# w2 read as four neighbouring rows to a partition, and the hidden activations turned with a stride of four

## The chip, the cores and the metric

The kernel runs on one core of one Trainium2 chip. The metric is the device time of one execution in microseconds (us), lower is better. The core's engines are TensorE (PE; its weight loads are listed apart as PEld), VectorE (DVE), ScalarE (ACT), GpSimd (POOL) and SyncE (SP), which here only issues transfers; 16 DMA engines move data between HBM and the on-chip memory SBUF. TensorE writes its results into PSUM.

## The reference, cut to what matters

The program is one decoder layer: attention and gated linear attention share a projection, then comes a mixture of experts, then a gated per-layer embedding. The change lies in the mixture of experts alone, for 512 tokens with 1024 features, 32 experts, 4 experts a token:

```python
def clamped_swiglu(hid):
    x_glu = jnp.minimum(hid[..., ::2], SWIGLU_LIMIT)
    x_lin = jnp.clip(hid[..., 1::2], -SWIGLU_LIMIT, SWIGLU_LIMIT)
    return x_glu * jax.nn.sigmoid(SWIGLU_ALPHA * x_glu) * (x_lin + 1.0)
...
    def expert_block(args):
        xb, e = args
        hid = xb @ w1[e] + b1[e]                    # 1024 -> 2048
        return clamped_swiglu(hid) @ w2[e] + b2[e]  # 1024 -> 1024
```

The second product is a sum over the 1024 hidden features. A sum can be taken in any order, so row f of `w2` only has to meet column f of the activations; on which partition and in which step of the sum they meet is free.

## The kernel before, in words

The expert part is a loop over 32 blocks, one for each expert with up to 96 token rows (`CAP`); in these inputs no expert needs a further block. All of w1 and w2 of an expert (12 MB) is streamed from HBM in 12 chunks of 1 MB, each 128 partitions by 2048 numbers. Chunks 0 to 3 and 6 to 9 are w1, chunks 10 and 11 are the first half of w2 (hidden features 0 to 511), and chunks 4 and 5 are the second half of the w2 of the expert before. SP issues the loads (L370) into a ring of six slots; the load of a chunk is issued once DVE has finished with the chunk six places ahead of it.

Each chunk goes through three engines. ACT rounds it to the upper part (`split_hi`, L703), DVE makes the rest, chunk minus upper part (`split_lo`, L1398), and both parts go to `HL`, a ring of four. PE then multiplies (w1 at L1063, w2 at L1091): for each of the chunk's two 128-row pieces it does three products (upper activations by upper weights, upper by rest, rest by upper), each in two halves of 512 columns, so 12 matmuls a chunk and 144 a block. The activations are what is loaded into the PE array, the weights of the model stream past.

Between the products DVE and ACT form the SwiGLU result `HIDr` (96 token rows by 1024 features, written by L1419 in two halves). PE turns each half in `turn_hidden` (L1098): four transposes, in each of which a 96 x 128 piece of `HIDr` is the array's load and the 96 x 96 identity streams past. The result is 128 features by 96 tokens. ACT copies it (L733, `HIDTh`) and DVE makes its rest (L1423, `HIDTl`); L1091 then uses piece f of `HIDTh` with piece f of w2. PE takes its work in a fixed order: chunks 0, 1, turn the second half of the block before, chunk 2, turn the next tokens (`turn_x`, L1051), chunk 3, bias, chunks 4, 5, then chunks 6, 7, turn the first half, chunks 8, 9, biases (L1072, L1079), chunks 10, 11.

Of the kernel before, what the change touches and what calls it, by code (L numbers as in the profile page):

```python
# [14 lines left out]
P = 128  # L15
# [12 lines left out]
CAP = 96  # L28
# [9 lines left out]
WRING = 6  # L38
# [4 lines left out]
def hybrid_layer(nc, x, p, g_mix, w_in, w_gla_gate, b_gla_gate, g_gla_norm, w_out, g_ffn, w_router, b_router,  # L43
                 w1, b1, w2, b2, w_ple_gate, w_ple_proj, g_ple, g_final, out):
    ctx = ExitStack()
    with ctx:
        def sb(name, shape, dt=F32):
            return ctx.enter_context(nc.sbuf_tensor(name, shape, dt))

        def sem(name):  # L50
            return ctx.enter_context(nc.semaphore(name))
# [6 lines left out]
        def scope(*shapes):  # L58

            with ExitStack() as held_here:  # L60
                return [held_here.enter_context(nc.sbuf_tensor(name, shape, dt)) for name, shape, dt in shapes]
# [9 lines left out]
        def in_w(at, *shape):  # L71
# [32 lines left out]
        ident = sb("ident", [P, P])  # L104
# [70 lines left out]
        BB, HIDr, HIDTh, HIDTl, T1, T2, SIG, _, XG, XTh, XTl, sel, _, W45 = scope(  # L175
            ("BB", [2 * NE, 3 * D], F32R),
            ("HIDr", [CAP, D], F32),
            ("HIDTh", [P, NC, CAP], F32R), ("HIDTl", [P, NC, CAP], F32R),
            ("T1", [CAP, 512], F32), ("T2", [CAP, 512], F32), ("SIG", [CAP, 512], F32),
            ("skip4", [P, 256], F32),  # L180
            ("XG", [CAP, D], F32),
            ("XTh", [P, NC, CAP], F32R), ("XTl", [P, NC, CAP], F32R),
            ("sel", [2 * NE, CAP], F32R),
# [3 lines left out]
        def w_slot(k):  # L187
            s = k % WRING
            return W[:, s * 2048:(s + 1) * 2048] if s < 4 else W45[:, s - 4]
# [8 lines left out]
        ps = ctx.enter_context(nc.psum_tensor("ps", [P, 8, 512], F32))  # L198
# [8 lines left out]
        w_in_s = [sem(f"w_slot_in{s}") for s in range(WRING)]  # L207
# [154 lines left out]

        def load_chunk(sp, b, k, e):
            if k in (4, 5, 10, 11):
                f = 512 + 256 * (k - 4) if k < 6 else 256 * (k - 10)
                src = w2[0, bass.ds(e, 1), f:f + 256, :]
            else:
                c, n = 256 * (k % 6), 1024 * (k // 6)
                src = w1[0, bass.ds(e, 1), c:c + 256, n:n + 1024]
            sp.dma_start(w_slot(k).rearrange("p (c n) -> p c n", c=2),  # L370
                         src.rearrange("o (c p) n -> p (o c) n", p=P)).then_inc(w_in_s[k % WRING], 16)

        def load_expert(sp, b, e, before_e):
            for k in range(NK):
                sp.wait_ge(w_lo, b * NK + (k - 7))
                load_chunk(sp, b, k, before_e if k in (4, 5) else e)

        def extra_blocks(eng, body):

            n = eng.value_load(tab[0:1, NEXTRA + 1:NEXTRA + 2], min_val=0, max_val=NEXTRA)  # L380
            with eng.If(n > 0):
                with eng.Fori(0, n) as i:
                    body(i)
            return n
# [4 lines left out]
        def _(sp):  # L389
# [28 lines left out]
            for k in range(4):  # L418
                load_chunk(sp, 0, k, 0)
# [3 lines left out]
            for k in range(6, 10):  # L423
                sp.wait_ge(w_lo, k - 5)
                load_chunk(sp, 0, k, 0)
# [409 lines left out]
        def _(pe):  # L835
# [4 lines left out]
            for c in range(NC):  # L840
                if c >= 4:
                    pe.wait_ge(at_lo, c - 3)
                for t in range(NT):
                    if c == 0:
                        pe.wait_ge(xs_ready, t + 1)
                    last = pe.transpose(ps[:, c % 4, t * P:(t + 1) * P], xs[:, t, c * P:(c + 1) * P], ident[:])
# [18 lines left out]
            for i, (name, _) in enumerate(CH):  # L865
                if name == "v":

                    pe.wait_ge(kt_ready, 2)
                    for hp in range(2):
                        g = GRP["ktok"] + hp  # L870
                        pe.wait_ge(proj_out, g - 3)
                        for t in range(NT):
                            last = pe.transpose(ps[:, g % 4, t * P:(t + 1) * P], ktail[:, hp, t * P:(t + 1) * P], ident[:])
                        last.then_inc(proj, 1)
                    pe.wait_ge(proj_out, GRP["ktok"] + 2)
                    for c in range(7):
                        t, r = c // 2, GC * (c % 2)
                        bank, at = 4 + c % 2 + 2 * (t // 2), 256 * (t % 2)
                        for h in range(GH):
                            lo = 64 * (h % 2)  # L880
                            last = pe.matmul(ps[lo:lo + 64, bank, at + (h // 2) * P:at + (h // 2 + 1) * P],
                                             ktok[r:r + GC, t, h * 64:(h + 1) * 64], vg[r:r + GC, t, h * P:(h + 1) * P],
                                             start=True, stop=True)
                        last.then_inc(kv_done, 1)
                for j in range(4):
                    g = GRP[name] + j
                    pe.wait_ge(proj_out, g - 3)
                    for c in range(NC):
# [8 lines left out]
                        for m, (l, r) in enumerate(pairs):  # L897
                            last = pe.matmul(ps[:, g % 4], l, r, start=(c == 0 and m == 0), stop=(c == NC - 1 and m == 2))  # L898
# [41 lines left out]
            for t in range(NT):  # L940
# [6 lines left out]
                for h in range(GH):  # L947
                    last = pe.matmul(ps[:, 1, h * P:(h + 1) * P], kd[:, h // 2, tt], qz[:, h, tt], start=True, stop=True)
                last.then_inc(a_done, 1)
                for i in range(MH + 2):  # L950
# [12 lines left out]
                    if 1 <= i <= MH:  # L963
# [5 lines left out]
                        for k in range(t + 1):  # L969
                            last = pe.transpose(ps[:, 6 + u % 2, k * P:(k + 1) * P], Pm[:, u % 4, k * P:(k + 1) * P], ident[:])  # L970
                        last.then_inc(pt_done, 1)
                    if i >= 2:

                        h = i - 2
# [4 lines left out]
                        for k in range(t + 1):  # L979
                            last = pe.matmul(ps[:, 0, h * 64:(h + 1) * 64], PTs[:, u % 2, k * P:(k + 1) * P], v_[:, k, h * 64:(h + 1) * 64],  # L980
                                             start=(k == 0), stop=(k == t))
                        last.then_inc(pv_done, 1)
                    if i == 2:

                        pe.wait_ge(a_out, t + 1)
                        for h in range(GH):
                            for e in range(2):
                                c = 2 * t + e
                                pe.matmul(ps[e * GC:(e + 1) * GC, 1, h * P:(h + 1) * P], qz[:, h, c * GC:(c + 1) * GC], st[:, c, h // 2],
                                          start=True, stop=False)  # L990
                            last = pe.matmul(ps[:, 1, h * P:(h + 1) * P], AT[:, h * P:(h + 1) * P], vg[:, t, h * P:(h + 1) * P],
                                             start=False, stop=True)
# [5 lines left out]
                for c in range(4):  # L998
                    last = pe.transpose(ps[:, 2, c * P:(c + 1) * P], ON[:, c * P:(c + 1) * P], ident[:])
# [5 lines left out]
                for c in range(4):  # L1005
                    last = pe.transpose(ps[:, 2, c * P:(c + 1) * P], OMS[:, c * P:(c + 1) * P], ident[:])
# [10 lines left out]
            for c in range(2):  # L1017
                for t in range(NT):
                    last = pe.transpose(ps[:, 4 + c, t * P:(t + 1) * P], prow[:, t, c * P:(c + 1) * P], ident[:])
# [4 lines left out]
            last = pe.matmul(ps[:, 7, 0:NT * NE], before[:], Mk[:], start=False, stop=True)  # L1024
# [17 lines left out]
            for a in range(NT * TOPK):  # L1042
                last = pe.matmul(ps[0:CAP, 4, 0:NTAB], ohJ[:, a, :], ohB[:, a, :], start=(a == 0), stop=(a == NT * TOPK - 1))
# [51 lines left out]
            def turn_hidden(b, h):  # L1095
                pe.wait_ge(hid_ready, b * 2 + (h + 1))
                for f in range(4):
                    last = pe.transpose(ps[:, 2 * h, f * CAP:(f + 1) * CAP], HIDr[:, (4 * h + f) * P:(4 * h + f + 1) * P], ident[0:CAP, 0:CAP])  # L1098
                last.then_inc(th_done, 1)

            def expert_block(b, first=False):
                w1_chunk(b, 0)
                w1_chunk(b, 1)
                if not first:
                    turn_hidden(b - 1, 1)
                w1_chunk(b, 2)
                turn_x(b + 1)
                w1_chunk(b, 3)
                add_b1(b, 0)
                if not first:  # L1110
                    for j in range(2):
                        w2_chunk(b - 1, 1, j, 4 + j, chunks(b, 4 + j))
                w1_chunk(b, 6)
                w1_chunk(b, 7)
                turn_hidden(b, 0)
                w1_chunk(b, 8)
                w1_chunk(b, 9)
                add_b1(b, 1)
                add_b2(b, first)
                w2_chunk(b, 0, 0, 10, chunks(b, 10))  # L1120
                w2_chunk(b, 0, 1, 11, chunks(b, 11))
# [5 lines left out]
            with pe.Fori(1, NE) as b:  # L1127
                expert_block(b)
            n = extra_blocks(pe, lambda i: expert_block(i + NE))
            turn_hidden(n + (NE - 1), 1)  # L1130
            for j in range(2):
                w2_chunk(n + (NE - 1), 1, j, 4 + j, (n + NE) * NK + (j - 1))
# [14 lines left out]
            for t in range(NT):  # L1147
# [3 lines left out]
                for n in range(2):  # L1151
                    for c in range(NC):
                        last = pe.matmul(ps[:, 2 + 2 * (t % 2) + n], actT[:, c, t * P:(t + 1) * P], wpg[:, n, c],  # L1153
                                         start=(c == 0), stop=(c == NC - 1))
# [367 lines left out]
```

## Time and profile before

| what | value |
|---|---|
| median of 3 runs | 1683.21 us (1681.07 to 1687.1) |
| the profiled execution | 1683.0 us |
| its span on the core | 1681.2 us |
| mean granted clock of TensorE | 0.961 of full speed |
| PE busy | 1589.6 us, 95% of the span |
| DVE busy | 1266.6 us, 75% |
| ACT busy | 990.0 us, 59% |
| expert loop | from about 410 us to about 1591 us of the span |

The busy time of an engine is the time in which one of its instructions runs. A busy PE need not be PE at its peak: matmuls overlap, and what counts is the step from one to the next. The chain is the list of work that set the end, followed back from the last instruction.

### The profile page before, as it was taken

The numbers are of one execution on the slowest core, as the hardware profiler recorded it, in microseconds if no ns is written. First come the engines' busy times: TensorE is split into PE (matmuls) and PEld (weight loads), VectorE is DVE, ScalarE is ACT, GpSimd is POOL, SyncE is SP. The second block draws the span as 40 slices with busy tenths as digits, with TensorE's granted clock in tenths as the row PEclk, the third lists the DMA queues.
The fourth block names the chain that finished last, engine by engine and source line by source line (L and its number), as shares of the span: only waits on it lengthen the run. The fifth ranks groups of instructions, "written<-read, shape, count | busy, mean of one in ns | idle before, by whom it ended". The sixth has DMA issues, their size and how long they took to land.

```text
span 1681.2 us, 20035 instructions
## 1 busy us (share of the span) xinstructions
PE 1589.6 (95%) x6953; PEld 1073.8 (64%) x6953; DVE 1266.6 (75%) x1031; ACT 990.0 (59%) x880; POOL 125.3 (7%) x114
## 2 busy tenths in 40 slices
PE   5999899976999999999999999999999999999777
PEld 3887556543666666666666666666666666666533
DVE  4422233335999999998999999999999999999554
ACT  5422222222777777777777777777777777777411
POOL 4000000002100000000000000000000000000070
PEclk9999688977999999999999999999999999999979
DMA  4128300055999999999999999999999999999571
GB/s 155 50 100 288 122 13 13 0 181 185 335 382 372 368 367 359 359 364 366 374 371 360 364 358 360 371 371 370 361 359 362 364 371 369 370 359 356 212 274 50
DMA packets 132513, 482.96 MB, mean 287 GB/s; under 512 B 9219, under 2 KB 9766, under 8 KB 132422
## 3 DMA queue, kind: packets, MB, share of 16 engines
q1 hardware_dynamic: 121222, 444.04, 72.1%
q0 software_dynamic: 6112, 21.52, 4.0%
q10 hardware_dynamic: 5152, 17.04, 2.7%
q8 instruction: 17, 0.28, 0.1%
q14 instruction: 10, 0.08, 0.0%
HBM read 455.44 MB, written 27.13 MB: 287 GB/s over the span
## 4 chain that ended last, share of the span: by engine, by line
PE 92%; DVE 2%; issue 2%; ACT 2%; DMA 1%; POOL 1%; SPq 0%; ACTq 0%; POOLq 0%; DVEq 0%
PE ps L1063 42%; PE ps L1091 22%; PE ps L898 8%; PE ps L913 4%; PE ps L1153 3%; PE ps L1072 2%; PE ps L958 1%; PE ps L1051 1%; PE ps L1098 1%; PE ps L1079 1%; PE ps L980 1%; PE ps L1035 1%; PE ps L970 1%; PE ps L932 1%; PE ps L852 1%
## 5 line engine op out<-in xcount | busy, mean ns | idle before, releaser
L1398 DVE TENSOR_TENSOR HL<-W,HL 128x2048 fp32r<-128x2048 f32 x384 | 875.5, 2288 | 93.4 <-ACT HL L703 85.9
L703 ACT ACTIVATE HL<-W 128x2048 fp32r<-128x2048 f32 x384 | 735.1, 1916 | 226.4 <-PE ps L1063 115.1
L1063 PE MATMUL ps<-HL,XTh 128*96 128x512 f32 x2048 | 562.2, 396 | 3.1 <-DVE XTl L1394 2.0
L1063 PEld LDWEIGHTS ps<-HL,XTh 128*96 128x96 f32 x2048 | 323.8, 162 | 134.2 <-issue 2.2
L1063 PE MATMUL ps<-HL,XTl 128*96 128x512 f32 x1024 | 319.6, 393 | 0.0
L1091 PE MATMUL ps<-HL,HIDTh 128*96 128x512 f32 x1024 | 283.5, 398 | 1.3 <-DVE HIDTl L1423 1.3
L1091 PEld LDWEIGHTS ps<-HL,HIDTh 128*96 128x96 f32 x1024 | 160.7, 162 | 91.9 <-issue 28.7
L1063 PEld LDWEIGHTS ps<-HL,XTl 128*96 128x96 f32 x1024 | 164.7, 161 | 70.7
L1091 PE MATMUL ps<-HL,HIDTl 128*96 128x512 f32 x512 | 160.4, 394 | 0.0
L540 POOL DMA_INDIRECT XG<-f_rows,tokix x33 | 58.3, 1767 | 1058.5 <-PE ps L1051 1058.2
L1091 PEld LDWEIGHTS ps<-HL,HIDTl 128*96 128x96 f32 x512 | 82.6, 161 | 35.4
L1197 DVE TENSOR_TENSOR PWl<-wst,PWh 128x1024 fp32r<-128x1024 f32 x24 | 29.8, 1252 | 71.7 <-ACT PWh L590 71.1
L913 PE MATMUL ps<-wst,actT 128*128 128x512 f32 x128 | 68.1, 674 | 7.2 <-DVE H L1249 6.7
L1284 DVE SCALAR_TENSOR_TENSOR M<-dist,ps 128x128 f32<-128x128 f32 (+3 forms) x32 | 15.6, 486 | 78.2 <-PE ps L958 78.2
L733 ACT ACTIVATE HIDTh<-ps 128x384 fp32r<-128x384 f32 x64 | 31.5, 492 | 57.2 <-PE ps L1098 57.2
L651 ACT ACTIVATE M<-M,nmax 128x128 f32<-128x128 f32 (+3 forms) x32 | 17.9, 561 | 77.4 <-DVE nmax L1287 77.4
L1153 PE MATMUL ps<-wpg,actT 128*128 128x512 f32 x128 | 58.0, 613 | 0.7 <-ACT actT L818 0.7
L744 ACT ACTIVATE XTh<-ps 128x768 fp32r<-128x768 f32 x32 | 26.0, 811 | 49.0 <-PE ps L1072 45.3
L913 PEld LDWEIGHTS ps<-wst,actT 128*128 128x128 f32 x128 | 24.9, 208 | 42.8 <-issue 42.8
L594 ACT ACTIVATE W<-ps 128x512 f32<-128x512 f32 x20 | 11.9, 593 | 67.7 <-PE ps L898 67.7
L1419 DVE TENSOR_TENSOR HIDr<-T,SIG 96x512 f32<-96x512 f32 x64 | 44.0, 688 | 5.0
L1153 PEld LDWEIGHTS ps<-wpg,actT 128*128 128x128 f32 x128 | 24.9, 198 | 31.2 <-issue 30.1
(231 smaller groups left out, 1428.5 us busy)
## 6 DMA issues: line engine op xcount, KB each, us to landing
W<-in_w_dram SPq DMA_DIRECT2D x384, 1024.0 KB, 7.9
wst<-in_w_in_dram SPq DMA_DIRECT2D x6, 2048.0 KB, 7.8
y_rows<-actT ACTq DMA_DIRECT2D x32, 384.0 KB, 6.1
y_rows<-M SPq DMA_DIRECT2D x1, 8064.0 KB, 40.6
H<-in_x_dram SPq DMA_DIRECT2D x8, 512.0 KB, 6.5
wst<-in_w_out_dram SPq DMA_DIRECT2D x2, 2048.0 KB, 16.3
wpg<-in_w_ple_gate_dram SPq DMA_DIRECT2D x2, 2048.0 KB, 9.6
f_rows<-M ACTq DMA_DIRECT2D x4, 512.0 KB, 2.9
```

The lines of the kernel that those rows point to most:

```text
L540: pool.indirect_dma_start(XG[:], None, f_rows, bass.IndirectOffsetOnAxis(ap=tokix[:, b:b + 1].bitcast(U32), axis=0)).then_inc(xg_in, 16)
L703: act.activation(HL[:, k % HRING, 0], w_slot(k), ACT.Copy).then_inc(w_hi, 1)
L733: act.activation(HIDTh[:, 4 * h:4 * h + 4], ps[:, 2 * h, 0:4 * CAP].rearrange("p (f j) -> p f j", f=4), ACT.Copy).then_inc(hth_out, 1)
L898: last = pe.matmul(ps[:, g % 4], l, r, start=(c == 0 and m == 0), stop=(c == NC - 1 and m == 2))
L913: last = pe.matmul(ps[:, 3], actT[:, c, t * P:(t + 1) * P], wst[:, n, c], start=(c == 0), stop=(c == NC - 1))
L1063: last = pe.matmul(ps[0:CAP, 2 * h + n], xt[:, c], HL[:, s, part, cc * 1024 + n * 512:cc * 1024 + (n + 1) * 512], start=(c == 0 and xt is ...
L1072: last = pe.matmul(ps[0:CAP, q], sel[:], BB[:, q * 512:(q + 1) * 512], start=False, stop=True)
L1091: last = pe.matmul(ps[0:CAP, 4 + n], ht[:, f], HL[:, s, part, ff * 1024 + n * 512:ff * 1024 + (n + 1) * 512], start=False, stop=(f == NC - ...
L1153: last = pe.matmul(ps[:, 2 + 2 * (t % 2) + n], actT[:, c, t * P:(t + 1) * P], wpg[:, n, c], start=(c == 0), stop=(c == NC - 1))
L1197: dve.tensor_tensor(PWl[:, c], wst[:, 0, c], PWh[:, c].bitcast(F32), ALU.subtract).then_inc(p_lo, 1)
L1398: dve.tensor_tensor(HL[:, k % HRING, 1], w_slot(k), HL[:, k % HRING, 0].bitcast(F32), ALU.subtract).then_inc(w_lo, 1)
L1419: dve.tensor_tensor(HIDr[:, h * 512:(h + 1) * 512], T2[:], SIG[:], ALU.mult).then_inc(hid_ready, 1)
```

## The change

The two w2 chunks of a half were two runs of 256 rows each, and within a chunk partition p held rows p and p + 128 of its run. Now a half of w2 (512 rows) is seen as 128 groups of four neighbouring rows; partition p belongs to group p, and the first chunk brings rows 4p and 4p + 1 of it, the second rows 4p + 2 and 4p + 3. A partition's share of a chunk is now one run of 8 KB in HBM where it was two of 4 KB. To meet these rows, transpose f of a half takes columns f, f + 4, f + 8, ... of that half of `HIDr`, where it took 128 neighbouring ones. The order of instructions on every engine, their number, the tiles in SBUF, the waits and the w1 loads are as they were.

```diff
         def load_chunk(sp, b, k, e):
             if k in (4, 5, 10, 11):
-                f = 512 + 256 * (k - 4) if k < 6 else 256 * (k - 10)
-                src = w2[0, bass.ds(e, 1), f:f + 256, :]
+
+                f, r = (512, 2 * (k - 4)) if k < 6 else (0, 2 * (k - 10))
+                src = w2[0, bass.ds(e, 1), f:f + 512, :].rearrange("o (p r) n -> p o r n", r=4)[:, :, r:r + 2, :].rearrange("p o r n -> p o (r n)")
+                sp.dma_start(w_slot(k).unsqueeze(1), src).then_inc(w_in_s[k % WRING], 16)
             else:
                 c, n = 256 * (k % 6), 1024 * (k // 6)
                 src = w1[0, bass.ds(e, 1), c:c + 256, n:n + 1024]
-            sp.dma_start(w_slot(k).rearrange("p (c n) -> p c n", c=2),
-                         src.rearrange("o (c p) n -> p (o c) n", p=P)).then_inc(w_in_s[k % WRING], 16)
+                sp.dma_start(w_slot(k).rearrange("p (c n) -> p c n", c=2),
+                             src.rearrange("o (c p) n -> p (o c) n", p=P)).then_inc(w_in_s[k % WRING], 16)
...
                 for f in range(4):
-                    last = pe.transpose(ps[:, 2 * h, f * CAP:(f + 1) * CAP], HIDr[:, (4 * h + f) * P:(4 * h + f + 1) * P], ident[0:CAP, 0:CAP])
+                    last = pe.transpose(ps[:, 2 * h, f * CAP:(f + 1) * CAP], HIDr[:, h * 512 + f:(h + 1) * 512:4], ident[0:CAP, 0:CAP])
                 last.then_inc(th_done, 1)
```

## Rows read from the trace of the kernel before

**Rows 1.** The page's slices of the span: busy tenths in 40 equal slices.

```profile
span 1681.2 us, 20035 instructions
PE   5999899976999999999999999999999999999777
DVE  4422233335999999998999999999999999999554
DMA  4128300055999999999999999999999999999571
```

**Rows 2.** Busy time, granted clock, DMA share and GB/s of two stretches of the loop.

```profile
core 0: us, PE busy (x) PEld busy (x) DVE busy (x) ACT busy (x) POOL busy (x), PEclk, DMA share, GB/s
600.00:800.00 200.00, 200.00 (x910) 137.18 (x908) 184.34 (x125) 145.57 (x110) 10.43 (x6) 1.00 1.00 364
```

**Rows 3.** Chain of one block, 902 to 939 us: start, length, what.

```profile
902.39 5.53 PE ps L1063 x24
907.93 0.33 PE ps L1098 x4
908.26 5.53 PE ps L1063 x24
...
914.88 5.70 PE ps L1091 x24
...
926.12 0.33 PE ps L1098 x4
...
939.00 5.53 PE ps L1063 x24
```

**Rows 4.** Waits between 600 and 1500 us: total us, times, longest.

```profile
ACT HL L703 <- PE ps L1063: 81.9, 99, 1.5
ACT HL L703 <- PE ps L1091: 72.5, 98, 1.1
DVE HL L1398 <- ACT HL L703: 59.0, 75, 1.2
```

**Rows 5.** All instructions of line 1098: duration ns min/median/max.

```profile
L1098 PEld LDWEIGHTS ps<-ident,HIDr x256: 137/141/143, 431.0 to 1579.5; 96*128 96x128 f32 x128
L1098 PE MATMUL ps<-ident,HIDr x256: 242/245/248, 431.2 to 1582.5; 96*128 96x96 f32 x128
```

**Rows 6.** Chain of the attention part: four transposes with 128 streaming columns.

```profile
301.39 0.44 PE ps L970 x4
```

**Rows 7.** Groups of lines, 300 to 1580 us: busy us, mean ns of one.

```profile
L913 PEld LDWEIGHTS ps<-wst,actT 128*128 128x128 f32 x56 | 10.1, 189 | 18.1 <-issue 18.1
```

**Rows 8.** Two reductions on DVE, in order of time: start us, us.

```profile
369.12 1.06 DVE L1330 TENSOR_REDUCE Mk<-M 128x128 f32<-128x512 f32 x1
379.24 0.69 DVE L1371 TENSOR_REDUCE Bs<-M 128x16 f32<-128x512 f32 x1
```

**Rows 9.** The load of a w2 chunk 11, and ACT's use of it.

```profile
L370 SPq DMA_DIRECT2D W<-in_w_dram x1: 373/373/373, 931.3 to 931.3; - x1
DMA to landing us min/median/max: 9.9/9.9/9.9
945.29 1.91 ACT L703 ACTIVATE HL<-W 128x2048 fp32r<-128x2048 f32 x1
```

**Rows 10.** DMA just after the loop's start, columns as in rows 2.

```profile
468.00:476.00 8.00, 8.00 (x37) 5.30 (x36) 7.32 (x5) 5.52 (x6) 0.00 (x0) 1.00 1.03 414
476.00:484.00 8.00, 8.00 (x36) 5.57 (x36) 7.96 (x9) 6.30 (x5) 0.00 (x0) 1.00 1.02 408
```

**Rows 11.** The page's transfers: packets of all, and the weights' loads.

```profile
DMA packets 132513, 482.96 MB, mean 287 GB/s; under 512 B 9219, under 2 KB 9766, under 8 KB 132422
W<-in_w_dram SPq DMA_DIRECT2D x384, 1024.0 KB, 7.9
```

**Rows 12.** The projections of the first part, chain, and L898 in a window (PE, PEld, clock, DMA share, GB/s).

```profile
89.90 35.94 PE ps L898 x154
100.00:140.00 40.00, 35.50 (x153) 28.32 (x152) 1.00 0.42 143
```

**Rows 13.** Chain at the start of the loop and behind it.

```profile
401.12 5.50 DMA XG<-f_rows,tokix
1579.76 2.79 issue
1584.06 7.32 PE ps L1091 x24
1621.26 13.73 PE ps L1153 x32
```

## The prediction

> **What bounds the kernel now.** I read the page's slices first. From the eleventh slice to the thirty-seventh PE, DVE and DMA all stand at 9 [rows 1], so three resources look full at once and the slices can't say which of them sets the pace. The stretches of the loop separate them: in 200 us PE is busy for 200.00, DVE for 184.34, ACT for 145.57, at a granted clock of 1.00, and the DMA engines show a share of 1.00 at 364 GB/s [rows 2]. A DMA share of 1.00 only says that some packet is always under way. What decides is who waits. The waits of the loop have ACT waiting for PE (81.9 and 72.5 us in all) and DVE waiting for ACT, and no wait of ACT for a load [rows 4]. The chain says the same: it runs through one block from 902.39 to 939.00 us on PE alone, 36.61 us a block, with no link through a transfer or another engine [rows 3]. So in the loop PE's own sequence is the time; anything else counts only when it makes PE wait.
>
> **The change part by part: the transposes.** They are on the chain. The four of one half take 0.33 us, so a step of about 82 ns each, twice a block [rows 3]; there are 256 of them, so 64 groups of four [rows 5]. The change leaves their number, size and place, and alters only how a group's array loads read `HIDr`: a number every 16 bytes where they were side by side. No PE instruction in this trace reads with such a stride, so the cost has to be bounded.
>
> First, how much cover has a load? Four transposes whose loads are as wide (128 columns) but whose streaming side is 128 and not 96 take 0.44 us, 110 ns each [rows 6]. The step grows with the streaming side while the load stays, so today the streaming matmul sets the step and the load is hidden in it: it takes 82 ns at most. How long does it really take? A load is recorded at 141 ns here [rows 5], and the f32 load of a plain matmul, as many columns, at 189 ns [rows 7]; the difference, 48 ns, is close to one clock of 2.4 GHz for each of 128 columns (53 ns). I read that as one clock a column for the transpose's load, 53 ns plus latency, and two clocks for the plain one, 107 ns plus latency. These two are estimates from the rows named.
>
> Lower end: the strided load stays under 82 ns and costs nothing. A gain I exclude, since the streaming side sets the step and is untouched. Upper end: the nearest strided read of SBUF in the trace is on DVE. The reduction at L1330 reads 512 numbers with 128 bytes between neighbours in 1.06 us, that at L1371 reads 512 side by side in 0.69 [rows 8], so 0.72 ns more a number, of which part may be its 128 results against 16. For 128 numbers that is 92 ns more a load. On top of 82 ns it is all exposed.
>
> Only three loads of a group can be exposed: the first runs under the 512-column matmul ahead, whose step is 5.53 / 24 = 230 ns [rows 3], and the load behind the last transpose is that of a w1 chunk, not strided. So 3 x 64 = 192 loads. Upper end: 192 x 92 ns = 17.7 us. Between ends this far apart I go by the row nearest to the case, L913's load, the same engine at two clocks a column: if a read that finds each number apart goes at half the rate, the load takes 107 ns, the step grows from 82 to 107 ns, and the cost is 192 x 25 ns = 4.8 us. I take this value.
>
> The Trainium skill speaks against the change here ("Advanced Engine Details and Errata", SBUF Cachelines): SBUF has lines of 16 bytes, at least two accesses have to hit a line for full rate, and each access in another line costs. With 16 bytes between numbers every access is in a new line. The page gives no size; DVE's strided reduction [rows 8] points the same way. A second rule I don't use as it stands: "TensorE: Matmul & The Clock Gate", LDWEIGHTS, gives columns / 1.2 ns, 107 ns for these 128 columns. The trace disagrees for transposes, since four of them would then take 0.43 us and take 0.33 [rows 3]; were it true, doubling it would cost 192 x (213 - 107) ns = 20 us.
>
> Behind the transposes stand ACT's copy (L733) and DVE's rest (L1423), needed by chunks 10 or 4 only 24 matmuls later (over 5.5 us); 0.1 us of delay there vanishes.
>
> **The loads.** 4 of 12 chunks are w2, so 128 of the 384 loads of 1 MB [rows 11]. At 4 KB each has 256 packets, 32,768 in all; as 8 KB packets it would be 16,384. Whatever that saves is hidden: the last w2 chunk of a block is issued at 931.3, lands 9.9 us later at 941.2, and ACT takes it at 945.29 [rows 9], 4.1 us later. Faster loads make that gap wider and nothing starts sooner, since nobody waits for them [rows 4]. So 0 us. If loads got slower, there is cover of two kinds: the 4.1 us, and throughput. A block moves 364 GB/s x 36.61 us = 13.3 MB [rows 2, 3], of which 12 x 1.05 MB are the weights. Just after the start the DMA engines moved 408 to 414 GB/s [rows 10], so a block's traffic fits in 32.5 us and 4.1 us a block are free.
>
> At the ends of the loop: block 0's start hangs on the first gather of tokens (5.50 us) [rows 13], and w2's first loads are queued behind four w1 chunks; the second half of the last block is behind PE's wait of 2.79 us for its own inputs. I count 0 for both.
>
> **The sum** is made against the profiled execution, 1683.0 us (a span of 1681.2 and 1.8 around it), which is 0.2 us under the median 1683.21. 1683.0 + 4.8 + 0 = 1687.8 us.
>
> **The rivals.**
> A: the strided load is still hidden under the 82 ns step. For it: 29 ns of room by my estimate of 53. Against it: strided reading on DVE has a price [rows 8]. Time 1683.0. In this case the change is worth nothing, since the load was never waited for. Whether packets really become 8 KB or are still cut at 4 KB makes no difference to it or to the forecast.
> B: the forecast, 1687.8.
> C: the load costs more than double. With four clocks a column it is 213 ns and the cost 192 x 131 ns = 25 us, so 1708; DVE's excess gives 17.7 us, 1700.7. Against it: on DVE a number cost 0.72 ns more, and three more clocks of 2.4 GHz would be 1.25. It decides as soon as a load passes 108 ns.
> D: the w2 loads become slow, for instance because a source of 8 KB out of every 16 KB, or a longer packet, moves worse, and DMA takes over as the bound. The point: 4.2 MB of a block take 10.2 us at 411 GB/s and may take 14.3 before the 4.1 us are used, so their rate must fall below 293 GB/s. At 250 GB/s the block is 2.5 us longer: 32 x 2.5 = 80 us, 1763. Against it: w1 chunks already come with a pitch of twice their run, and the loop runs at 364 GB/s with them.
> E: faster. A matmul of 512 columns steps by 230 ns where one of 512 in f32 takes two clocks a column and 2 ns (13.73 us / 32 = 429) [rows 13]; against 213 ns that is 17 ns more for each of 4608 matmuls, 78 us. If that came from DMA writes disturbing PE's reads, a sixth fewer packets could return 13 us: 1670. Against it: in the first part the same kind of matmul steps by 35.94 / 154 = 233 ns with the DMA share at 0.42 [rows 12], so the 17 ns are not the transfers'.
>
> **How the numbers follow.** B 0.40, A 0.33, C 0.13, E 0.10, D 0.04. The predicted time is B's, 1687.8. A and B with the scatter of runs (1681.07 to 1687.1 before) span 1679 to 1692; C's cheaper half starts at about 12 us, so I set the upper end at 1695, which leaves out most of C, D and most of E, together about 0.2. About 0.3%, 5.05 us, is what a measurement of this kernel can tell from no change. B's 4.8 us lie at that bound, so it gives 0.24 to "same" and 0.16 to "slower"; A goes to "same", C and D to "slower", E to "faster". Faster 0.10, same 0.57, slower 0.33.
>
> **What the profile after would show.** The transposes of line 1098 are the test: in the chain a group of four takes 0.33 us if A holds, about 0.41 if B does, 0.6 to 0.7 if C does, and the load's record grows from 141 ns to about 195 for B. The block grows from 36.61 to 36.76 us for B. The chain stays on PE, with no wait of ACT for a load; a wait there, or a DMA link in the chain, would be D. The packets under 8 KB fall from 132,422 to about 99,650 if the runs stay whole, and w1's matmuls keep 5.53 us for 24; if they don't, E is at work and my account of the loop is wrong. The prediction is wrong if the time leaves 1679 to 1695, and its mechanism is wrong if the time moves with the groups of transposes unchanged.

## The result, and the profile after

| | before | changed |
|---|---|---|
| median (5 runs each) | 1683.21 us (1681.07 to 1687.1) | 1689.51 us (1687.86 to 1691.29) |
| profiled execution | 1683.0 us | 1689.51 us |
| its span | 1681.2 us | 1687.7 us |
| PE busy | 1589.6 us | 1595.6 us |

The changed kernel is slower: ratio 1.0037, 95% interval 1.0023 to 1.005. The forecast was 1687.8 us in 1679 to 1695, with 0.57 on "within 0.3%" and 0.33 on "slower"; the ratio lies just beyond 0.3%, on the side that had the smaller chance of the two (its interval still takes in 1.003).

The chain of the same block in the changed kernel answers to [rows 3] (start, length, what; lines moved by two, so 1100 is the transposes' 1098):

```profile
904.72 5.54 PE ps L1065 x24
910.26 0.45 PE ps L1100 x4
910.71 5.53 PE ps L1065 x24
...
917.32 5.70 PE ps L1093 x24
...
928.57 0.45 PE ps L1100 x4
...
931.78 0.66 PE ps L1053 x8
...
941.54 3.46 PE ps L1065 x15
```

Every piece of the chain keeps its length to within 0.01 us but the two groups of transposes, 0.45 us where 0.33 stood. A block goes from 36.61 to 36.82 us. Two points of the chain 30 blocks apart give it to the third decimal; these are the starts of the token transposes, first in the kernel before, then in the changed one:

```profile
453.34 0.66 PE ps L1051 x8
1551.54 0.66 PE ps L1051 x8
```

```profile
453.12 0.66 PE ps L1053 x8
1557.72 0.66 PE ps L1053 x8
```

1098.2 us became 1104.6, so 36.607 and 36.820 us a block: 6.4 of the 6.5 us that the span grew lie between these two points. All the rest of the program together gives 0.1. The lines of the transposes themselves, answering to [rows 5]:

```profile
L1100 PEld LDWEIGHTS ps<-ident,HIDr x256: 197/209/221, 430.7 to 1585.9; 96*128 96x128 f32 x128
L1100 PE MATMUL ps<-ident,HIDr x256: 247/282/319, 430.9 to 1589.6; 96*128 96x96 f32 x128
```

The load's record (the duration that the profile gives it) went from 141 to 209 ns. The matmul behind it looks longer too (245 to 282), though it streams the same 96 columns: I read its record as including time spent waiting on the load, so the load is where to look. (In e5 below, where the strided load has a long matmul to hide under, the same record is 247 ns.) The packets, answering to [rows 11], and the loop's busy time, to [rows 2]:

```profile
DMA packets 116129, 482.96 MB, mean 286 GB/s; under 512 B 9219, under 2 KB 9766, under 8 KB 99654
600.00:800.00 200.00, 200.00 (x906) 138.25 (x905) 183.27 (x125) 144.26 (x108) 10.49 (x6) 1.00 0.98 362
```

The runs stayed whole (16,384 packets fewer). The weight traffic is what it was, the DMA share went from 1.00 to 0.98, and PE is as full as before, of slightly dearer work.

### The profile page after: what moved, and what is told of

Same layout as the page of the kernel before. It is cut to its first block, busy times and chain, and to the rows that moved or that the text cites. A ratio compares the mean times of both kernels' runs of the same rounds, so it can differ in the third digit from the quotient of the medians.

```text
span 1687.7 us, 20035 instructions
## 1 busy us (share of the span) xinstructions
PE 1595.6 (95%) x6953; PEld 1085.2 (64%) x6953; DVE 1267.1 (75%) x1031; ACT 990.3 (59%) x880; POOL 129.3 (8%) x114
## 2 busy tenths in 40 slices
DMA packets 116129, 482.96 MB, mean 286 GB/s; under 512 B 9219, under 2 KB 9766, under 8 KB 99654
## 4 chain that ended last, share of the span: by engine, by line
PE 91%; issue 2%; DVE 2%; ACT 2%; POOL 1%; DMA 1%; SPq 0%; ACTq 0%; POOLq 0%; DVEq 0%
PE ps L1065 42%; PE ps L1093 22%; PE ps L900 8%; PE ps L915 4%; PE ps L1155 3%; PE ps L1074 2%; PE ps L1100 2%; PE ps L960 1%; PE ps L1053 1%; PE ps L982 1%; PE ps L1081 1%; POOL rstd L535 1%; PE ps L972 1%; PE ps L934 1%; PE ps L1037 1%
## 5 line engine op out<-in xcount | busy, mean ns | idle before, releaser
L1100 PEld LDWEIGHTS ps<-ident,HIDr 96*128 96x128 f32 x256 | 41.0, 209 | 7.3
```

## The experiments

Two theories stood against each other at first. S: the strided array load is exposed under the transposes' step. L: the 8 KB runs of w2 cost the time. Each ratio is to the kernel before on the same chip; "a block" is taken over 30 blocks as above, and repeats far better than the whole time does, which scatters by several us between runs: the four runs whose transposes still stand in groups and load neighbours in the hidden activations and the tokens alike (before, e2, e4, e10) lie at 36.594 to 36.623 us. So a difference of under 0.03 us a block should not be read.

**e1, the stride alone.** Against the kernel before:

```diff
-                    last = pe.transpose(ps[:, 2 * h, f * CAP:(f + 1) * CAP], HIDr[:, (4 * h + f) * P:(4 * h + f + 1) * P], ident[0:CAP, 0:CAP])
+                    last = pe.transpose(ps[:, 2 * h, f * CAP:(f + 1) * CAP], HIDr[:, h * 512 + f:(h + 1) * 512:4], ident[0:CAP, 0:CAP])
```

> The kernel before with the transposes of the hidden activations alone turned with a stride of four columns; w2's loads stay two runs of 4 KB a partition, so w2's rows meet other features than they should. Theory S (the strided array load takes about 120 ns, passes the 82 ns step of a transpose and is exposed three times a group): all of the change's loss is here, ratio 1.003 to 1.005 to the kernel before (about 1689.5 us), a group of four transposes 0.45 us in the chain, the load's record 209 ns. Theory L (the loss comes from the 8 KB runs of w2): ratio 1.000, although the groups of transposes may look the same as in the changed kernel.

Measured: ratio 1.0031 (1.0016 to 1.0045), a block 36.827 us, packets as before. Its transposes:

```profile
L1098 PEld LDWEIGHTS ps<-ident,HIDr x256: 197/209/222, 427.5 to 1582.9; 96*128 96x128 f32 x128
```

**e2, the loads alone.** Against the changed kernel, the same line the other way round:

```diff
-HIDr[:, h * 512 + f:(h + 1) * 512:4]
+HIDr[:, (4 * h + f) * P:(4 * h + f + 1) * P]
```

> The changed kernel with w2 loaded as four neighbouring rows a partition, but the transposes taking 128 neighbouring columns as before, so w2's rows meet other features than they should. Theory S: ratio 1.000 within 0.001, groups of transposes 0.33 us, 116,129 packets. Theory L: ratio 1.003 to 1.004. If 8 KB runs brought any gain that the transposes then ate, this run is below 1.000.

Measured: ratio 0.9993 (0.998 to 1.0006), 116,129 packets, a block 36.607 us, the same to the third decimal as before. Together with e1 this settles the first question: the whole of the loss comes with the stride, and whole 8 KB runs neither cost nor bring anything that can be measured in a loop that does not wait for its loads.

**e3, two neighbouring rows, a stride of two.** Against the changed kernel:

```diff
-                f, r = (512, 2 * (k - 4)) if k < 6 else (0, 2 * (k - 10))
-                src = w2[0, bass.ds(e, 1), f:f + 512, :].rearrange("o (p r) n -> p o r n", r=4)[:, :, r:r + 2, :].rearrange("p o r n -> p o (r n)")
+                f = 512 + 256 * (k - 4) if k < 6 else 256 * (k - 10)
+                src = w2[0, bass.ds(e, 1), f:f + 256, :].rearrange("o (p r) n -> p o (r n)", r=2)
...
-HIDr[:, h * 512 + f:(h + 1) * 512:4]
+HIDr[:, h * 512 + 256 * (f // 2) + f % 2:h * 512 + 256 * (f // 2 + 1):2]
```

> w2's chunks are again runs of 256 rows, but a partition holds rows 2p and 2p + 1 (one run of 8 KB), and the transposes take every second column, 8 bytes apart. The whole is computed. Theory S with its reading that the price hangs on numbers that share a 16-byte piece of SBUF: two of them share one here, the load stays near 141 ns, a group takes 0.33 us and the ratio is 1.000. Rival (any stride costs the same): load 209 ns, group 0.45 us, ratio 1.004. In between (price in proportion to the pieces touched, 64 against 32 and 128): load about 160 to 165 ns, which is still under the step, ratio 1.000.

Measured: ratio 1.0027 (1.0016 to 1.0039), a block 36.807 us.

```profile
L1099 PEld LDWEIGHTS ps<-ident,HIDr x256: 198/208/223, 430.7 to 1585.4; 96*128 96x128 f32 x128
```

My own reading fell here. Numbers 8 bytes apart, two to a 16-byte piece, are as dear as numbers 16 bytes apart (0.200 us a block against 0.213, a difference inside the scatter).

**e7, a stride of three.** Against the kernel before, `HIDr[:, h * 512 + f:h * 512 + f + 382:3]`.

> The kernel before with the transposes taking every third column, 12 bytes apart; w2 as before, so its rows meet other features than they should. With side by side 141 ns and the changed kernel's stride of four 209 ns: by the pieces of 16 bytes that a load touches (96 of 128) the record would be about 190 ns; if any stride over one costs the same, 209 ns and a group of 0.45 us.

Measured: ratio 1.0037 (1.0022 to 1.0052), the load's median 202 ns, a group 0.43 us in the chain, a block 36.793 us. The record lies between the 190 and the 209 ns of the two readings and nearer to the second, and strides of 2, 3 and 4 give 208, 202 and 209 ns: no growth with the number of 16-byte pieces touched (64, 96, 128).

**e10, side by side, but one column on.** Against the kernel before, the 128 neighbouring columns start 4 bytes further on (the last of a group 4 bytes further back).

> The kernel before with each transpose of the hidden activations reading 128 neighbouring columns, but from one column further on (the last of a group from one further back), so that the row of 512 bytes no longer starts on a multiple of 16 bytes; features meet other rows of w2 than they should. If side by side is what counts, nothing changes: load 141 ns, block 36.61 us. If the fast load needs an aligned start, load about 205 ns and block 36.8 us.

Measured (one run): a block 36.594 us.

```profile
L1098 PEld LDWEIGHTS ps<-ident,HIDr x256: 138/140/144, 435.4 to 1583.6; 96*128 96x128 f32 x128
```

So what makes the cheap load is that the columns are neighbours; a start 4 bytes off changes nothing.

**e8 and e9, eight strided token transposes.** Against the kernel before, at line 1051 (e8, then e9):

```diff
-XG[:, c * P:(c + 1) * P]
+XG[:, c:D:NC]
...
-XG[:, c * P:(c + 1) * P]
+XG[:, (c // 4) * 512 + c % 4:(c // 4 + 1) * 512:4]
```

> The kernel before with the token transposes of line 1051 taking every eighth column, 32 bytes apart; w1 as before, so its rows meet other features than they should. 8 transposes a group, 33 groups, so 7 x 33 = 231 exposed loads. If beyond one number for each 16 bytes the distance no longer matters: load 209 ns, 39 ns exposed each, the group grows from 0.66 to 0.93 us, 9 us in all, ratio 1.005. If the price goes on growing with the distance, the load is above 209 ns and the ratio above 1.008.

> The kernel before with the token transposes of line 1051 taking every fourth column of a half, as the changed kernel does with the hidden activations; w1 as before, so its rows meet other features than they should. So far four strided loads cost 0.107 us a group, eight at stride eight 0.184. If the price is one exposed load each (7 against 3), eight at stride four cost 7/3 of 0.107, 0.25 us, and the block takes 36.86 us; if a group has a price of its own (about 0.03) beside 0.025 a load, the block takes 36.80; if the distance mattered, eight against four columns, it would show in the load's record (206 ns at stride eight, 209 at four in the other transposes).

Measured: e8 ratio 1.0032 (1.0016 to 1.0047), a block 36.791 us, a group 0.86 us where 0.66 stood: neither the 0.93 us nor the growth that I had named. e9 (one run): a block 36.867 us, (1556.13 - 450.13) / 30. Its group and loads:

```profile
929.40 0.92 PE ps L1051 x8
```

```profile
L1051 PEld LDWEIGHTS ps<-ident,XG x264: 195/219/226, 403.3 to 1556.7; 96*128 96x128 f32 x132
```

Seven exposed loads cost 0.260 us a block, 37 ns each; the changed kernel's six cost 0.213, 36 ns each. So the count of one less than the group fits, and a price of a group by itself, which wanted 36.80 us, is out. The starts of e9's loads in the trace say the same without any sum: inside the group they lie 120 ns apart (median), where the kernel before has 82. Stride eight is cheaper, not dearer: 26 ns each, 110 ns from load to load, with a record of 206 against 219 ns. Why stays open. The differences between strides of 2, 3 and 4 (33, 31 and 36 ns a load) are no larger than the scatter.

**e5, e6 and e11, the transposes taken apart.** Against the changed kernel (e5) and the kernel before (e6), the transposes of a group are issued inside chunk 1 or 7:

```diff
+                            m += 1
+                            if m == 12:
+                                last.then_inc(piece_used, 1)
+                            if turn is not None and m % 3 == 0:
+                                turned_f = turn_one(turn[1], m // 3 - 1)
```

In e11 the last two lines read `if turn is not None and m % 6 == 0:` and issue two transposes each time.

> The changed kernel with the four strided transposes of a group no longer back to back: they stand behind the 3rd, 6th, 9th and 12th matmul of the chunk ahead (chunk 1 or 7), so that each strided load runs under a 512-column matmul (230 ns). Block 0's first group stays as it was. The whole is computed. Theory S: a load of about 120 ns is hidden there, so this runs as e6 does (ratio of the two 1.000), 6 us under the changed kernel if spreading itself costs nothing. Rival (a strided read slows the array or its streaming side wherever it stands): 6 us above e6.

> The kernel before, with its transposes (neighbouring columns) spread as in e5. The whole is computed. Theory S takes from it only what spreading costs by itself: near 1.000 to the kernel before; four switches between the two kinds of array load instead of one may cost up to 0.1 us a group, 1.003.

> As e5, but the four strided transposes stand in two pairs, behind the 6th and the 12th matmul of the chunk ahead. The whole is computed. One load of a pair is under a 512-column matmul, one under an 82 ns transpose. By 35 ns for each exposed load: 2 a group, 4 a block, 36.62 + 0.14 = 36.76 us a block; e5 with none exposed has 36.66, the changed kernel with 3 a group 36.82.

Measured: e5 ratio 1.0015 (1.0003 to 1.0026), a block 36.660 us; e6 ratio 1.0008 (0.9991 to 1.0024), a block 36.620; e11 (one run) a block 36.767. The chain of e5, one strided transpose at a time, then of e6, one side by side transpose at a time, and then of e11:

```profile
921.30 0.08 PE ps L1057
921.38 0.70 PE ps L1071 x3
922.08 0.09 PE ps L1057
922.17 0.70 PE ps L1071 x3
```

```profile
920.50 0.09 PE ps L1055
920.58 0.69 PE ps L1069 x3
921.28 0.08 PE ps L1055
921.36 0.69 PE ps L1069 x3
```

```profile
910.13 0.20 PE ps L1057 x2
910.33 1.40 PE ps L1071 x6
911.73 0.20 PE ps L1057 x2
```

Alone behind a 512-column matmul a strided transpose adds 0.08 to 0.09 us, what a side by side one adds; a pair adds 0.20, not 0.17. Against e6, the loss goes from 0.200 us a block with three exposed loads a group (36.820 - 36.620) to 0.147 with one exposed a pair (four a block) and to 0.040 with none. So exposure is most of it, but the 0.040 us, 5 ns for each of the eight strided transposes of a block, are there without any. They sit in the matmuls: the 512-column matmul just ahead of a transpose, the one that the transpose's load runs under, takes 237 ns on average from its start to the next in e5 and 231 in e6. So the rival of e5's expectation, a strided read that slows the streaming side, is there too, at a fifth of the size that it wanted. With 5 ns set aside for each strided load under a 512-column matmul (two a block in the changed kernel, four in e11, one in e9), an exposed load costs 32 ns, 32 ns and 36 ns. In whole times e5 and e6 can't be told apart (their intervals overlap); the blocks and the chain are what carries this.

**e4, the stride moved to DVE.** Against the changed kernel, besides the transposes' line as in e2:

```diff
-                dve.tensor_tensor(HIDr[:, h * 512:(h + 1) * 512], T2[:], SIG[:], ALU.mult).then_inc(hid_ready, 1)
+                dve.tensor_tensor(HIDr[:, h * 512:(h + 1) * 512].rearrange("p (f g) -> p g f", f=4), T2[:].rearrange("p (g f) -> p g f", f=4),
+                                  SIG[:].rearrange("p (g f) -> p g f", f=4), ALU.mult).then_inc(hid_ready, 1)
```

> The changed kernel with the stride moved from PE to DVE: the product that makes HIDr (line 1421) reads its inputs in groups of four and writes each number 512 bytes from the next, so that the transposes take 128 neighbouring columns. The whole is computed. Theory S: groups 0.33 us, ratio 1.000; DVE's product may grow from 0.69 us to at most about 1.4 us, twice a block, 1.4 us beside DVE's free 2.9 us a block, and hidden. Rival: DVE has no such room, since chunks wait for it one by one: then PE waits for DVE (line 1400) and the ratio is above 1.005.

Measured: ratio 0.9998 (0.9986 to 1.001), a block 36.623 us, groups at 0.33 us.

```profile
L1421 DVE TENSOR_TENSOR HIDr<-T,SIG x64: 1091/1105/1117, 431.3 to 1578.5; 96x512 f32<-96x512 f32 x64
```

DVE's product grew from 688 to 1105 ns, 0.83 us a block, and DVE's wait for ACT between 600 and 1500 us fell by 15.9 us, of the 20 that the slower product took there:

```profile
DVE HL L1400 <- ACT HL L705: 43.1, 50, 1.2
```

It was 59.0 us [rows 4]. An engine with waits to spare took the stride for nothing.

**e12, the stride in the large matmuls.** Against the kernel before, at line 1063:

```diff
-                            last = pe.matmul(ps[0:CAP, 2 * h + n], xt[:, c], HL[...],
+                            last = pe.matmul(ps[0:CAP, 2 * h + n], xt[:].rearrange("p c j -> p (c j)")[:, c:NC * CAP:NC], HL[...],
```

> The kernel before with the array loads of all w1 matmuls (line 1063, 96 columns, 3072 of them) reading every eighth column of XTh and XTl instead of 96 neighbours; the features meet other rows of w1 than they should. If the stride takes away a fast way of loading that only the transposes have (141 against 189 and 162 ns), these loads stay at 162 ns and the block at 36.61 us. If every strided load becomes slower by the same 60 to 70 ns, the record grows to about 225 ns, still hidden under the step of 230, and the block stays too; if the time grows, the load has passed the step.

Measured: ratio 1.022 (1.0202 to 1.0238), a block 37.693 us. A load of the kernel before, then of e12, and e12's chain:

```profile
L1063 PEld LDWEIGHTS ps<-HL,XTh x2048: 159/161/280, 410.2 to 1571.6; 128*96 128x96 f32 x187
```

```profile
L1063 PEld LDWEIGHTS ps<-HL,XTh x2048: 253/262/288, 411.1 to 1606.7; 128*96 128x96 f32 x187
```

```profile
917.41 5.76 PE ps L1063 x24
923.16 0.33 PE ps L1098 x4
923.50 5.82 PE ps L1063 x24
```

The step of the 512-column matmul grew from 230 to 240 ns (5.76 / 24): 96 matmuls a block, 0.96 us of the 1.09 that a block grew; most of the rest stands behind the three groups of transposes. The expectation named a reason for the case that the time grows, the load has passed the step, and the record of 262 ns seems to bear it out. The trace does not. Behind the four transposes of a group the first w1 load has only an 82 ns transpose above it, so a load of more than 230 ns would stick out there by some 150 ns. The run of 24 behind the transposes takes 5.82 us where the other takes 5.76, only 0.06 more. These are the loads there, the first row from the first w1 load on, the second from the next one on; e12, then the kernel before:

```profile
923.25 0.90 PEld L1063 LDWEIGHTS ps<-HL,XTh 128*96 128x96 f32 x4
923.41 0.75 PEld L1063 LDWEIGHTS ps<-HL,XTh 128*96 128x96 f32 x3
```

```profile
926.21 0.71 PEld L1063 LDWEIGHTS ps<-HL,XTh 128*96 128x96 f32 x4
926.29 0.40 PEld L1063 LDWEIGHTS ps<-HL,XTh 128*96 128x96 f32 x2
```

The second load starts 0.16 us after the first (0.08 before), and the first matmul ends about 0.1 us late. By that a strided load of 96 columns takes some 160 to 180 ns (an estimate from these rows), which fits under 230. A second sign: the load has nearly the same record behind the transposes (255 ns) as under the long matmuls (262), so it is not much slower there. So the reading that fits is the one that e5 left over: a 512-column matmul becomes slower while a strided load runs under it, by 6 ns in e5 and by 10 here. No run separates this further, and why it happens stays open.

## Why the prediction was right, point by point

The size was near and the mechanism held: 1687.8 forecast, 1689.51 measured; +4.8 forecast, +6.5 in the profiled execution.

- **PE's own sequence is the time, and the loads of w2 are worth nothing either way.** Shown: e2 has the block of before to the third decimal with 16,384 packets fewer. Rival D (slow w2 loads) falls with it. Rival E does too: with 16,384 packets fewer 24 matmuls of w1 still take 5.53 us, so the 17 ns above the streaming time do not go with the number of packets. The bytes moved are the same in all runs, so whether they matter is not shown here; the 233 ns of [rows 12] at a DMA share of 0.42 speak against it.
- **The cost is in the three loads of each group that only a transpose covers.** Shown: e1 has the loss alone, e5 removes 0.160 of 0.200 us by giving each load a longer matmul to hide under, and one (e11), three (changed) and seven (e9) exposed loads a run of transposes cost 36 to 37 ns each (32 to 36 without what the hidden load of each run costs). I had put that hidden load at nothing. It is about 5 ns (e5), 0.3 us in the whole kernel.
- **The cover is 82 ns, and the load then takes about 107.** This is the term that was mis-sized. With 36 ns exposed the load takes about 118 ns (120 from load to load in e9) where I had two clocks a column, 107; 192 x 36 = 6.9 us stands where 192 x 25 = 4.8 stood. The record grew by 68 ns, and the doubling of an estimated 53 would give 53. I can't say what the extra quarter is. That the whole came within 2 us is in part luck: 25 ns is the difference of two larger figures, one of them a guessed rate, and 11 ns in the load's length already change the term by nearly half.
- **Rival A** (still hidden, 1683.0) is refuted by the 0.45 us group, **rival C** (four clocks) by its size: it wanted 0.6 to 0.7 us.
- **The price from the nearest rows.** I took the PE row with two clocks a column over DVE's strided reduction, whose 92 ns a load lay too high. The choice was better than the reason I gave with it. I had the price hang on each number finding itself alone in its piece of SBUF, and cited the Trainium skill for it ("Advanced Engine Details and Errata", SBUF Cachelines). e3 contradicts that for TensorE's load: with two numbers in each 16 bytes it still pays in full, 208 ns. What the runs support is simpler: for these transposes neighbouring columns load in under 82 ns, also from a start 4 bytes off (e10), and with every stride tried (2, 3, 4, 8) the load takes 108 to 120. By my estimate of 53 ns for neighbours that is about half the rate; no run measures the 53.
- **The chances.** 4.8 us lay just inside the 5.05 that I called the bound of "same", so I leaned to "same"; the 2 us that the term was short moved it across.

## What to carry to other kernels

A layout that makes a transfer tidier pays only where somebody waits for that transfer; here nobody did, and the price was sent to the one engine that had no slack. If a permutation must be made, let the engine with waits to spare make it while it writes (e4), not TensorE while it loads. And judge a longer array load by the matmul that it runs under: a transpose with 96 streaming columns hides 82 ns, a 512-column matmul hides all of the strided load but 6 to 10 ns, by which it gets slower itself. That is small for eight transposes a block and made the kernel 2.2% slower when all matmuls of w1 paid it (e12). And read how long a load takes from the distance of its start to the next where little covers it, not from its record: a record of 262 ns was a load of 160 to 180.

## What the runs showed of the hardware that I had not expected

- TensorE's array load of f32 data: neighbours 141 ns for a transpose's 128 columns, 199 to 219 ns with strides of 2, 3 or 4 and 206 with 8. A stride of 8 bytes is as dear as one of 16. From load to load, back to back, it is 82 ns for neighbours, where the streaming side sets the pace, and 120 with a stride of 4 (e9).
- In a matmul's load of 96 columns the same step from neighbours to stride eight costs 101 ns of record (161 to 262), and 3072 of these, nearly all under a 512-column matmul, made the kernel 2.2% slower.
- A 512-column matmul takes longer while a strided load runs under it: 240 ns instead of 230 (e12), 237 instead of 231 (e5 against e6).
- DVE's product of 512 numbers with strided inputs and output took 1105 ns instead of 688, 0.8 ns a number.
